# Attention levels issued in pairs, with the work between them in another order

## The reference, cut to what matters

```python
def encoder_trunk(x, ...):                       # a prompt of 512 and a sample of 1024 tokens, width 1024
    h = rms_norm(x, norm_mix)
    x = x + hybrid_mixer(h, ...)                 # 4 Fourier groups of 128 columns, 4 HGRN2 heads of 128
    h = rms_norm(x, norm_ffn)
    x = x + expert_choice_ffn(h, ...)            # 16 experts, each takes 1/8 of the tokens
    return rms_norm(x, norm_final)

# a head, forward (the backward direction is the same on flipped tokens)
k, logf = hgrn2_gates(z, lb)                     # decay per token and per channel
b = cumsum(logf)
o[t] = sum over s <= t of (q[t] . k[s] * exp(b[t] - b[s])) v[s]
y = rms_norm(o_fwd + o_bwd, out_norm) * silu(g)
```

## Time and profile before

| | |
|---|---|
| time, median of 3 launches | 2556.99 us (2556.1 to 2558.35) |
| the profiled execution's own time | 2552.32 us |
| its span (first to last instruction) | 2550.6 us |
| mean granted TensorE clock | 0.997 of full |
| PE busy / PE weight load busy | 2510.8 us (98%) / 2263.5 us (89%) |
| DVE / ACT / POOL busy | 1648.6 / 1359.3 / 327.1 us |

### The profile page before, as it was taken

One profiled execution on the slowest core, in us unless ns is written; L12 is line 12 of the kernel. 1 busy time (PEld: TensorE's weight loads), 2 busy tenths in 40 slices (PEclk: granted clock), 3 DMA queues, 4 the chain that ended last, 5 costly groups with the idle time before them and its releaser, 6 DMA issues.

```text
span 2550.6 us, 44352 instructions
## 1 busy us (share of the span) xinstructions
PE 2510.8 (98%) x18109; PEld 2263.5 (89%) x18109; DVE 1648.6 (65%) x1997; ACT 1359.3 (53%) x1627; POOL 327.1 (13%) x237
## 2 busy tenths in 40 slices
PE   7999999999999999999999999999999999999998
PEld 6777778787877999999999999999999999999997
DVE  6556565444387676767667676766767666676667
ACT  6435353434665555555555555555555555555556
POOL 3102020101120011020211202021020202102020
PEclk9999999999999999999999999999999999999999
DMA  4001010135447676675767767676676767667677
GB/s 159 26 22 55 2 55 10 57 137 198 173 144 273 231 256 239 228 261 211 268 228 251 247 235 251 226 259 234 251 249 235 248 221 256 236 234 258 225 259 282
DMA packets 63987, 503.08 MB, mean 197 GB/s; under 512 B 7536, under 2 KB 7920, under 8 KB 39568
## 3 DMA queue, kind: packets, MB, share of 16 engines
q1 hardware_dynamic: 48016, 448.84, 48.3%
q0 software_dynamic: 15872, 52.83, 7.0%
HBM read 464.42 MB, written 37.22 MB: 197 GB/s over the span
## 4 chain that ended last, share of the span: by engine, by line
PE 92%; DVE 3%; ACT 2%; DMA 1%; issue 1%; POOL 0%; SPq 0%; DVEq 0%; ACTq 0%; POOLq 0%
PE up_banks_b L2241 15%; PE up_banks_a L2241 15%; PE up_banks_b L2244 6%; PE up_banks_a L2244 6%; PE bank L64 5%; PE bank L66 5%; PE bank L65 5%; PE up_banks_b L2282 2%; PE up_banks_b L2280 2%; PE up_banks_b L2281 2%; PE up_banks_b L2279 2%; PE up_banks_a L2283 2%; PE up_banks_b L2283 2%; PE up_banks_a L2279 2%; PE up_banks_a L2282 2%; PE up_banks_a L2280 2%
## 5 line engine op out<-in xcount | busy, mean ns | idle before, releaser
L2009 DVE TENSOR_TENSOR big_lo<-wide,big_hi 128x4096 fp32r<-128x4096 f32 x189 | 836.3, 4425 | 410.2 <-ACT big_hi L1774 410.0
L1774 ACT CAST big_hi<-wide 128x4096 fp32r<-128x4096 f32 x190 | 690.3, 3633 | 515.8 <-PE up_banks_a L2241 240.8
L2241 PE MATMUL up_banks_b<-x_parts,big_hi 128*128 128x384 f32 x2016 | 574.3, 356 | 0.0
L2241 PE MATMUL up_banks_a<-x_parts,big_hi 128*128 128x384 f32 x1984 | 565.0, 356 | 1.0 <-DVE h_parts L2033 1.0
L2244 PE MATMUL up_banks_b<-x_parts,big_lo 128*128 128x192 f32 x1764 | 442.0, 251 | 0.0
L2244 PE MATMUL up_banks_a<-x_parts,big_lo 128*128 128x192 f32 x1736 | 435.0, 251 | 0.0
L2241 PEld LDWEIGHTS up_banks_b<-x_parts,big_hi 128*128 128x128 f32 x2016 | 365.3, 189 | 0.2
L2241 PEld LDWEIGHTS up_banks_a<-x_parts,big_hi 128*128 128x128 f32 x1984 | 359.4, 189 | 1.9 <-DVE h_parts L2033 1.2
L2244 PEld LDWEIGHTS up_banks_b<-x_parts,big_lo 128*128 128x128 f32 x1764 | 336.1, 191 | 0.0
L2244 PEld LDWEIGHTS up_banks_a<-x_parts,big_lo 128*128 128x128 f32 x1736 | 330.8, 191 | 0.6
L64 PE MATMUL bank<-big_hi,w_hi 128*128 128x512 f32 x576 | 236.5, 411 | 0.0
(11 more groups left out here) (345 smaller groups left out, 4177.9 us busy)
## 6 DMA issues: line engine op xcount, KB each, us to landing
wide<-in_expert_weights SPq DMA_DIRECT2D x190, 2048.0 KB, 7.7
w_raw<-in_w_heads SPq DMA_DIRECT2D x48, 256.0 KB, 2.8
x_in<-in_x SPq DMA_DIRECT2D x12, 512.0 KB, 4.0
x_d<-in_x POOLq DMA_DIRECT2D x12, 512.0 KB, 5.8
residual<-x_d POOLq DMA_DIRECT2D x12, 512.0 KB, 3.6
ffn_in<-h_and_xT_d POOLq DMA_DIRECT2D x12, 512.0 KB, 3.0
wide<-residual SPq DMA_DIRECT2D x12, 512.0 KB, 6.4
tab<-in_tables POOLq DMA_DIRECT2D x10, 512.0 KB, 7.3
```

The source lines that it names most:

```text
L1774: nc.scalar.copy(ahead.hi(c), raw[:, c % RAW]).then_inc(hi_done, 1)
L2009: nc.vector.tensor_tensor(ahead.lo(c), raw[:, c % RAW], ahead.hi(c).bitcast(F32), ALU.subtract).then_inc(lo_done, 1)
L2241: last = nc.tensor.matmul(out[:, 0:2 * CAP], hi, x[:, k], start=n == 0, stop=n == KT - 1, skip_group_check=True)
```

## The change

Levels now run in pairs (0,1), (2,3), (4,5), (6,7), in the odd slots. For that the keys have two tiles, `keys[0]` and `keys[1]`, and for even levels ACT gathers the queries too (tile `queries`), so that DVE can multiply on for the odd level before PE has run the even one. The gather is an event of its own (`prep`), and so is the copy of `near` (`near`). The work of a block is laid out anew around the pairs. `FILL` is now 1,2,1,2,1,2,1,0. The values are turned behind the last pair. `u` comes after the first slot's fill, in front of the first pair, and the updates begin in that slot. The DMA scratch in SBUF is halved from its default of 16384 to make room for the two tiles.

```diff
-        keys = sb("keys", [P, BLK])
+        keys = [sb(f"keys{i}", [P, BLK]) for i in range(2)]
+        queries = sb("queries", [P, BLK])
...
-        FILL, LAST_FILL = (1, 1, 1, 1, 1, 2, 2, 1), (2, 2, 2, 1, 1, 1, 1, 1)
+        FILL, LAST_FILL = (1, 2, 1, 2, 1, 2, 1, 0), (2, 2, 2, 1, 1, 1, 1, 1)
...
-                    s = 1 + i // 2
+                    s = i // 2
                     at_slot[s] += [("update", h, d, k, turns[d][k]) for k in pair for d in range(2)]
                     at_slot[s + 1] += [("inter", h, d, k, turns[d][k + 1]) for k in pair for d in range(2)]
                 f = 2 + (steps - 1) // 2
                 at_slot[f] += [("square", h, b) for b in blocks]
                 at_slot[f + 1] += [("root", h, blocks[0])]
-                at_slot[f + 2] += [("rstd", h, blocks[0])]
+                at_front[f + 2] += [("rstd", h, blocks[0])]
                 at_end[f + 2] += [(kind, h, b) for kind in ("rows", "out") for b in blocks]
             for s in range(8):
-                if n < NN:
-                    timeline.append(("level", n, s))
+                timeline += at_front[s]
+                if n < NN and s % 2 == 0:
+                    timeline.append(("prep", n, s + 1))
+                    if s == LEVELS - 1:
+                        timeline.append(("near", n))
+                elif n < NN:
+                    timeline += [("level", n, s - 1), ("level", n, s)]
+                    if s < LEVELS:
+                        timeline.append(("prep", n, s + 1))
+                if s:
+                    timeline += at_slot[s] + take_gates()
+                timeline += take_halves(FILL[s] if n < NN else LAST_FILL[s])
                 if s == 0 and n >= 1:
-                    timeline += [("u", n - 1, 0), ("u", n - 1, 1)]
-                timeline += at_slot[s] + take_gates()
-                timeline += take_halves(FILL[s] if n < NN else LAST_FILL[s]) + at_end[s]
+                    timeline += [("u", n - 1, 0), ("u", n - 1, 1)] + at_slot[0]
+                if s < 7 or n == NN:
+                    timeline += at_end[s]
             if n < NN:
-                timeline += [("intra", n), ("kt", n, 0), ("kt", n, 1)]
+                timeline += take_turn() + [("intra", n)] + at_end[7] + [("kt", n, 0), ("kt", n, 1)]
...
+            def rise(n, s):                      # the body of DVE's old level, up to the two products in kq
...
+                if s % 2 == 1:
+                    filled(dve, ("level", n, s))
+                else:
+                    prepared(dve, n, s)
...
-                elif kind == "level" and ev[2] >= 1:
+                elif kind == "level" and ev[2] % 2 == 1:
                     _, n, s = ev
...
+                    rise(n, s)
+                    for t in (s - 1, s):
+                        take_level(("level", n, t))
+                elif kind == "prep" and ev[2] % 2 == 1 and ev[2] > 1:
+                    rise(ev[1], ev[2] - 1)
...
-    nc = bacc.Bacc("TRN2", target_bir_lowering=False, num_devices=1)
+    nc = bacc.Bacc("TRN2", target_bir_lowering=False, num_devices=1, dynamic_dma_scratch_size=8192)
```

More of the change, by code:

```diff
@@ L320, in heads_phase, with take_turn @@
         to_gate = []
+        def take_turn():
+            return [stream.pop(0)] if stream and stream[0][0] == "vt" else []
         def take_halves(count):
             taken = []
-            while stream and (count or stream[0][0] == "vt"):
+            while stream and count:
                 count -= stream[0][0] != "vt"
@@ L512, in split_weights, with gather @@
                         weights.high(act, (h * NJ + j) * 2 + f)
[L514 to L521, removed]
+            def gather(out, n, left, right, level):
                 half = 1 << level
-                nc.scalar.copy(keys[:].rearrange("p (n two h) -> p n two h", two=2, h=half),
-                               halves(n % NB, KF, KB, level, 0, BLK)).then_inc(keys_ready, 1)
+                nc.scalar.copy(out[:].rearrange("p (n two h) -> p n two h", two=2, h=half),
+                               halves(n % NB, left, right, level, 0, BLK)).then_inc(keys_ready, 1)
             def take_projection(ev):
@@ L574, in _ @@
                     nc.scalar.copy(v_tok[:, n % NB], bank[MS][:]).then_inc(bank_read[MS], 1)
+                elif kind == "prep":
+                    _, n, s = ev
+                    if s == 1:
+                        act.wait_ge(kq_made, n + 1)
+                    else:
+                        act.wait_ge(kq_up, n * LEVELS + s - 1)
+                    if n >= 1 or s > 2:
+                        filled(act, ("level", n, s - 2) if s > 2 else ("level", n - 1, LEVELS + 1 - s))
+                    if s % 2 == 0:
+                        gather(queries, n, QB, QF, s - 1)
+                    gather(keys[s % 2], n, KF, KB, s - 1)
+                elif kind == "near":
+                    n = ev[1]
+                    act.wait_ge(intra_done, n)
+                    was_read(act, ("level", n, NEAR))
+                    for keys_of in STRIPS:
+                        nc.scalar.copy(scores[keys_of, :, keys_of], near[keys_of])
                 elif kind == "level" and ev[2] == 0:
@@ L581, in _ @@
                     nc.scalar.copy(near[:], near_view[i]).then_inc(bank_read[i], 1)
-                    gather_keys(n, 0)
-                elif kind == "level" and ev[2] < LEVELS:
-                    n = ev[1]
-                    gather_keys(n, ev[2])
-                    if ev[2] == NEAR + 1:
-                        i = fill_of[ev][0]
-                        act.wait_ge(intra_done, n)
-                        was_read(act, ("level", n, NEAR))
-                        for j, keys_of in enumerate(STRIPS):
-                            nc.scalar.copy(scores[keys_of, :, keys_of], near[keys_of])
-                        for j, keys_of in enumerate(STRIPS):
-                            queries = STRIPS[j ^ 1]
-                            copied = nc.scalar.copy(scores[keys_of, :, queries], bank[i][keys_of, :, queries])
-                        copied.then_inc(bank_read[i], 1)
+                elif kind == "level" and ev[2] == NEAR + 1:
+                    filled(act, ev)
+                    i = fill_of[ev][0]
+                    for j, keys_of in enumerate(STRIPS):
+                        other = STRIPS[j ^ 1]
+                        copied = nc.scalar.copy(scores[keys_of, :, other], bank[i][keys_of, :, other])
+                    copied.then_inc(bank_read[i], 1)
+                elif kind == "level" and ev[2] < LEVELS:
+                    continue
                 elif kind == "level":
@@ L836, in _ @@
                             first = c * P + j * STRIP
[L837 removed]
+                            k = (keys[s % 2] if s else k_sum)[:, first:first + STRIP]
                             if s == 0:
                                 qs = q[:, first:first + STRIP]
+                            elif s % 2 == 0:
+                                at = first if s <= NEAR else c * P + (j ^ 1) * STRIP
+                                qs = queries[:, at:at + STRIP]
                             elif s <= NEAR:
                                 qs = halves(b, QB, QF, s - 1, first, STRIP)
[L842 to L844 removed]
                             elif s == LEVELS:
```

80 lines of the change are left out of this document (43 added, 37 removed).

## The result

The changed kernel takes 2601.73 us in the median (2599.5 to 2607.32, four launches), against 2556.55 us (2554.19 to 2558.35) for the kernel before beside it: a ratio of 1.0189, 95% interval 1.0177 to 1.0201 (the quotient of the two medians is 1.0177, at its lower end). The prediction was 2598.9 us, with 0.93 on slower. The profiled execution took 2599.5 us, with a mean granted clock of 0.991. The other three launches had 0.989, 0.988 and 0.986 and took 2600.23, 2603.23 and 2607.32 us: what one launch differs from the next goes with the clock.

What follows compares the result with a forecast made beforehand. PE, busy 98% of the span, was taken as the bound; 43.1 us of waits less 7.5 of interruptions plus 6.3 of clock gave 41.9 us more, 2598.9 us on the median, range 2567 to 2614.

Steps and rivals of the forecast that it cites:

- Interruptions: PE switching from products to small matmuls and back: 34 fewer at 0.22 us each, a gain of 7.5 us.
- The cover in front of `intra`: Products behind level 7 gone, so `intra` waits for DVE's copy: 12.1 us in eight blocks, 1.9 in block 11.
- Blocks 3, 6 and 9: Level 7's copy comes late behind last gates, table load, root and `rstd`: 5.7 us lost in each, 17.1 in all.
- my signs of being wrong: `intra` 1 us after level 7; PE waiting at a pair for keys; or loss behind the heads at a POOL DMA.
- the stretch: Rival: DVE gates or multiplications lengthened while POOL makes the weights' rests, adding 7 to 14 us; above 2607 us, chance 0.14.
- `u`'s copies: Level 1 waits for ACT's copy of `u`: 3.5 us in seven blocks, 6.6 in 4, 7, 10, 0.9 in 1; 11.0 us.
- Block 12's `inter`: `inter` right behind `u` waits for the copy and four updates: 1.0 us, between 0 and 2.
- The keys of level 7: In blocks 1, 4, 7 and 10 `out` joins the path to these keys: nothing, up to 0.5 us a block.
- The clock: PE's clock falls to half rate at the long waits in blocks 3, 6 and 9: 6.3 us, bounds 0 and double.
- At nothing: Costed at no time: query gathers, pair-to-pair path, `out` waiting for `rows`, last projections, halved DMA scratch.
- The halved scratch: Smaller DMA scratch touches POOL's DMAs, issued long after their wait for data: nothing, at most a few microseconds.
- the path from pair to pair: Multiplications and gathers between pairs, about 6.8 us, hidden beneath 8.78 us of PE work: no cost.

Runs made afterwards that it cites:

- a_copy: Changed kernel with DVE's copy of level 7 into the scores ahead of its two last multiplications; 2592.15 us, ratio 1.0151 to the kernel before.
- a_pool: Changed kernel with GpSimd's rests of the weights held back until DVE's last multiplications in blocks 3, 6 and 9; 2597.51 us, ratio 1.0179 to the kernel before.
- a_keep: Changed kernel plus 10 unused products ahead of level 7 and 18 ahead of the values' turn in blocks 3, 6, 9; 2595.95 us, ratio 1.0165.
- a_rstd: Changed kernel with the norm's division (`rstd`) behind level 7's multiplications and copy again; 2600.81 us, ratio 1.0185 to the kernel before.
- b_scratch: Kernel before with only the DMA scratch halved to 8192; 2553.86 us, ratio 1.0002 to the kernel before.
- a_covers: Changed kernel with levels 0 and 1 unpaired, 12 products after each of levels 0 and 7, `rstd` behind level 7, odd-slot gates later; 2562.05 us, ratio 1.0032.

## Why the prediction was right

*The sign and the size.* Forecast 41.9 us above the median before, measured 45.2 on the medians beside each other (47.1 between the spans, 48.3 by the ratio). The terms below were off by between -1.9 and +4.6 us each, and in part these errors cancel; so far the closeness of the sum is luck.

*Interruptions, -7.5 us.* Right in kind, too small in size. No run undid this term alone, but two readings bear on it. From pair to pair PE takes 9.09 us (206.07 to 215.16) for two levels and 36 products, where two lone levels with them took 3.34 + 6.06 = 9.40: 0.31 us less for the joined level, and I had 0.22. And this is where the heads end, before and after:

```profile
556.19 0.45 PE L1411 MATMUL bank_d<-fourier_space 128*128 128x128 f32 x2
```

```profile
600.08 0.45 PE L1456 MATMUL bank_d<-fourier_space 128*128 128x128 f32 x2
```

That is 43.9 us later, with 45.4 us more waits and 7.8 lost, so 9.3 us were gained; worked out in the same way the nine kernels with 34 joined give 7.4 to 10.7. The account, which has 7.5, is within 1.5 us in nine of the ten kernels with pairs (in a_copy it is 3.7 too high) partly because of what it leaves out: behind the heads the changed kernel takes 3.2 us longer than the kernel before, and over all profiles that part scatters from 1993.7 to 1999.1 us.

*The cover in front of `intra`, 14.0 us in nine blocks.* Measured 12.8 (26.0 less 13.2 in blocks 3, 6 and 9), single waits of 1.26 to 1.85 us. Right, with one thing missing, which a_copy showed: ACT's half of level 7 is nearly as late as DVE's.

*Blocks 3, 6 and 9, 5.7 us each.* The mechanism was right, the size too small: 2.82 us for the keys (forecast 0.9) and 3.80 to 4.68 in front of `intra` (forecast 4.8), 21.6 in all against 17.1. From level 4's start `intra` was to begin at 16.3 us and began at 18.3. The mis-sized part of the term is the DVE rows for the last raise, which I priced at their undisturbed length; beside POOL they took 1.1 us more each, and a_pool, which removed it, has 0.67 us left in front of the keys. The wait for keys was also among my signs of being wrong, though the sum itself had 0.9 us of it: in these blocks the path between the pairs is longer than the 8.8 us of cover. I had the stretch among the rivals and not in the sum. The root started 0.02 us behind its load, at 220.72, as in the row used, and the load began as the last copy ended, at 219.42. The Trainium skill ("ScalarE: Activation LUTs", What ACT_TABLE_LOAD costs) adds a drain of about 1380 ns to the load; no row here shows one.

*`u`'s copies, 11.0 us.* Measured 9.1: in blocks 4, 7 and 10 2.08, 2.08 and 2.56 (forecast 2.2), in plain ones 0.18 to 0.29 (forecast 0.5). In block 1 it is 0.80 (forecast 0.9). The copy follows `u` closer than I read from the values' copy: at the start of block 3 it begins 0.10 us behind level 0 (184.33 against 184.23), where I had 0.36.

*Block 12's `inter`, 1.0 us.* `inter`'s five waits are 2.3 us: 0.7 in block 12, and 0.3 to 0.4 in each of blocks 1, 4, 7 and 10 behind the first pair, where I had none. The keys of level 7 cost 0.26 to 0.27 us each in blocks 1, 4 and 7, within the 0.5 that I allowed.

*The clock, 6.3 us.* Measured 7.8 in the profiled execution, 6.2 of it in blocks 3, 6 and 9, as said, and 1.6 behind the 2.56 us at 489 us. The other launches had a lower clock and took longer. On the whole time a_keep gives 2.6 to 6.1 us. The Trainium skill ("TensorE: Matmul & The Clock Gate", Why this matters for your kernels) warns of idle gaps between bursts; the trace agrees behind the 3.80 and 4.68 us, and the clock also fell behind waits shorter than the page speaks of. What I did not foresee is how little order there is in it: a_rstd, a_pool and a_copy have fewer waits than the changed kernel and lose 7 to 9 us more, though in a_copy the waits saved outweighed that. Why a wait of 1.28 us brings the clock down in one execution and 1.84 does not in another stays open.

*At nothing.* The halved scratch (b_scratch) and the path from pair to pair were rightly costed at nothing here; a_covers shows how near the latter is.

## What to carry to other kernels

Joining small pieces on a busy engine pays by the interruption (0.22 to 0.31 us here), but what stood between them was the cover of a chain on other engines: before it is moved, write down for each piece what must end under it, and in which blocks that chain is longest (here those that also work off a norm with its table load). Put instructions that only late work needs (`rstd`, `out`, GpSimd's rests) behind the raise that the next matmul needs: three such moves and one fill brought the ratio to the kernel before from 1.0189 to 0.9989. A wait can cost more than its length where it brings the clock down (here 7.8 us on top of 46.7), so don't expect every shortened wait to come back in time.

## What was not expected of the hardware

- Two DVE rows beside POOL's two `TENSOR_TENSOR` were 1.07 and 1.09 us longer (1.75 for 0.68, 1.26 for 0.17), and on the chain this cost 2.1 us of PE in each of three blocks.
- The clock fell to half behind waits of 1.28 us (a_pool, windows at 265 and 267.5 us: 0.87 and 0.50) and 1.85 (a_keep, 522 us), and held behind 1.28, 1.84 and 1.85 in the profiled execution of the changed kernel.
- Small products whose results nobody reads kept the clock at full through 6.6 us in which TensorE had nothing to do, and took no time of their own (9.22 us against 9.21).
